# Building the block Toeplitz matrix of a state-space mixer with selecting matmuls and ScalarE copies instead of on-chip transfers

## The chip, the cores and the metric

One core of one Trainium2 chip runs the whole program. The metric is device time in microseconds (us), the median over several executions. The granted TensorE clock has two levels, 2.4 GHz ("1.00" in the profile) and 1.2 GHz ("0.50").

## What is computed

One inference step of a two-layer decoder trunk over 512 prompt tokens and 8 sample tokens, width 1024, all in float32. Layer 0 is a diagonal complex state-space mixer (S5) and a mixture of 16384 tiny experts (PEER); layer 1 is latent attention and a second PEER. What matters here is the mixer and the modulation vectors:

```
mod = silu(c) @ w_mod + b_mod              # 9 rows of c, 16384 columns in all: 64 MB of weights
h   = rmsnorm(x) * (1 + scale) + shift
bu[l] = h[l] @ b_bar;  s[l] = lam_bar * s[l-1] + bu[l]      # 64 groups, 64 states, 16 inputs each
y[l]  = real(c_mat @ s[l]) + d_skip * h[l]
```

The recurrence is cut into 64 chunks of 8 tokens. Inside a chunk, y is a product of the chunk's inputs with a block Toeplitz matrix: for each of the 64 groups a 128 x 128 matrix whose block (s, t), 16 x 16, is the response K[t-s] of the group for t >= s, and zero for t < s. Between chunks only the state is carried.

## The kernel before

**The weight blocks.** `w_mod` is read in 32 blocks of 2 MB (numbers 0 to 31), each as two halves of 1 MB and a bias row of 2 KB, all issued by the SP queue (`mod_loads`, L785 and L787). A block has one of two slots (its number's parity, called b). The load of block n+2 into a slot is issued half by half, as TensorE finishes each half of block n (`s_modmm`). TensorE multiplies a block in `mod_pair` (L2469, 64 instructions; L2474 with the bias, 8), which waits for the whole block; ScalarE copies the 9 x 512 result out of PSUM (`mod_copy`, L1214, four pieces) and stores it to `mod_rows` in HBM.

**The rounds.** TensorE goes through a fixed list, `ROUNDS`: m (turns the input tables), s (turns the sample rows), u (turns the prompt rows), i (injections into the states), k (the responses: 16 groups each, into PSUM), y (the output). The 8 PSUM banks are two halves; a round waits until the round before it in its half was copied out. `MOD_AFTER` says after which round one weight block each is multiplied. Blocks 0 to 3 come before all rounds (`MOD_FIRST = 4`), 4 to 21 between them, and 22 to 31 after k3 in a loop of their own, with other places in SBUF (`MOD_ONE = 22`, `MOD_PLACES[1]`). Their load waits until round k3 is multiplied (`s_mm`). SP loads blocks 0 to 5 without regard to the rounds, then waits for the stored rows of blocks 0 to 3, reads these back, and goes on with block 6.

**The Toeplitz matrix.** `toep` lies where `MOD_PLACES[0]` lay, so it waits for block 21. GpSimd clears it (L1107, 128 x 8192) and then issues 32 transfers from SBUF to SBUF (L1112): for each of the 4 k rounds and each s of 8, the copied responses `ksb[r]` (16 partitions at partition 32r, 16 groups x 128 columns) go to partitions 16s to 16s+15, shifted right by 16s columns:

```
for s in range(TC):
    pool.dma_start(toep[GP * s:GP * (s + 1), RG * r:RG * (r + 1), GP * s:P],
                   ksb[r][:, :, 0:P - GP * s]).then_inc(s_toep, 16)
```

In all 2.36 MB, in 8192 contiguous pieces of 512 down to 64 bytes.

**After it.** VectorE copies the i rounds out (L1836 to L1841), then runs the scan over the chunks (up to L1913). When the scan, block 31 and the 32 transfers are done, VectorE (L1918) and ScalarE (L1284) place the states in `hx`, two copies each, and TensorE does the y rounds (L2535, L2536). The GLU, PEER, attention and the second PEER follow, with waits only on work of their own. GpSimd's gathers of expert rows (L1124) are the long part of the program.

Of the kernel before, what the change touches and what calls it, by code (L numbers as in the profile page):

```python
# [12 lines left out]
ACT = mybir.ActivationFunctionType  # L13
AX = mybir.AxisListType

P = 128
# [4 lines left out]
NB = 8  # L21
# [32 lines left out]
MOD_S5 = 4  # L54
MOD_FIRST = 4
MOD_ONE = 22
HALF_MOD = KD * MB // 2


def program(nc, a):  # L60

    with ExitStack() as ctx:
# [29 lines left out]
        SEL = o; o += NB  # L92
        EYE = o; o += 32
        SILU = o; o += KD * NC9
# [117 lines left out]
        s_tz = sem("chunk_pad_and_response_cleared")  # L212
        s_toep = sem("response_loaded")
        s_mm = sem("s5_round_products")
# [35 lines left out]
        def row_no(passes, stage, j):  # L250
# [3 lines left out]
                    if row_slot(q, m) == slot and not (passes is LOADS and (q, m) in NOT_LOADED)]  # L254
# [4 lines left out]
                  + [("i", 0), ("k", 0), ("m", 2), ("i", 1), ("k", 1), ("m", 3), ("i", 2), ("k", 2), ("i", 3), ("k", 3)]  # L259
                  + [("y", r) for r in range(NR)])  # L260
        WHO = {"u": "A", "k": "A", "m": "A", "i": "V", "s": "A", "y": "V"}
        MOD_AFTER = [("m", 0), ("m", 1), ("m", 1), ("s", 0), ("u", 0), ("u", 1), ("u", 2), ("u", 3), ("u", 3), ("k", 0),
                     ("m", 2), ("i", 1), ("k", 1), ("m", 3), ("i", 2), ("k", 2), ("i", 3), ("k", 3)]
        assert MOD_FIRST + len(MOD_AFTER) == MOD_ONE
        round_no = {key: n for n, key in enumerate(ROUNDS)}
# [500 lines left out]
        def _(sp):  # L766
            sp.dma_start(at(SILU, KD * NC9), a["c_t"]).then_inc(s_in, 16)
            sp.dma_start(at(IDENT, P + TOPK + NB + 32), a["consts"]).then_inc(s_in, 16)
            sp.dma_start(par, a["s5_par"][:, 0:NPAB]).then_inc(s_par, 16)
# [37 lines left out]
            for b in range(2):  # L807
                sp.wait_ge(s_modmm[b], NMB)
            sp.wait_ge(s_toep, 16 * TC * NR)
            sp.dma_start(hx[:, :, CH:CH + NB], a["state_x"]).then_inc(s_st0, 16)  # L810
# [285 lines left out]
        def _(pool):  # L1096
# [8 lines left out]
            for b in range(2):  # L1105
                pool.wait_ge(s_modmm[b], MOD_ONE)
            pool.memset(at(TOEP, G * P), 0.0).then_inc(s_tz, 1)  # L1107
            pool.wait_ge(s_tz, 3)
            for r in range(NR):
                wait_copied(pool, ("k", r))  # L1110
                for s in range(TC):
                    pool.dma_start(toep[GP * s:GP * (s + 1), RG * r:RG * (r + 1), GP * s:P],  # L1112
                                   ksb[r][:, :, 0:P - GP * s]).then_inc(s_toep, 16)

# [65 lines left out]
        def _(act):  # L1180
# [55 lines left out]
            act.wait_ge(s_ms, 1)  # L1236
            act.activation(stat[:, 8:13], stat[:, 8:13], ACT.Sqrt).then_inc(s_rt, 1)

            for key in ROUNDS[:round_no[("y", 0)]]:
                kind, r = key  # L1240
                if WHO[kind] == "V":
                    for pair in mods_between(key):
                        mod_copy(*pair, one=True)
                    continue
                act.wait_ge(s_mm, round_no[key] + 1)
                ps = half(key)
                if kind == "u":
                    for s in range(2):
                        ins = act.activation(
                            u2[64 * s:64 * s + 64, RG * r:RG * (r + 1), 0:CH].rearrange(  # L1250
                                "p (b g) c -> p b g c", b=4),
                            ps[0:64].rearrange("p b (g c) -> p b g c", g=4)[:, :, :, 64 * s:64 * s + 64], ACT.Copy)
                        if s == 0:
                            link(ins)
                elif kind == "s":
                    act.wait_ge(s_tz, 1)
                    turned = ps[:, 0:2].rearrange("p b n -> p (b n)")
                    link(act.activation(u2[0:GP, :, CH:CH + NB], turned[0:GP, NB * (TC - 1):NB * (TC - 1 + G)].rearrange(
                        "p (g b) -> p g b", g=G), ACT.Copy))
                    ins = act.activation(u2[96:P, :, CH + NB:UC], turned[96:P, 0:NB * G].rearrange(  # L1260
                        "p (g b) -> p g b", g=G), ACT.Copy)
                elif kind == "k":
                    ins = act.activation(ksb[r].rearrange("p (b g) m -> p b (g m)", b=4), ps[0:GP], ACT.Copy)
                else:
                    if r >= 2:
                        act.wait_ge(s_mm, round_no[("i", r - 2)] + 1)
                    if r == 0:
                        act.wait_ge(s_blp, 3)
                        act.wait_ge(s_lam, 16)
                    ins = act.activation(minb[r % 2].rearrange("p (b g) m -> p b (g m)", b=4), ps, ACT.Copy)  # L1270
                ins.then_inc(s_evA, 1)
                for pair in mods_between(key):
                    mod_copy(*pair, one=True)
                if kind == "s":
                    act.wait_ge(s_cn, 1)
                    act.activation(cl[0:64, :, 0, :], c_re[0:64], ACT.Copy).then_inc(s_clr, 1)
                    act.activation(cl[64:P, :, 0, :], c_im[64:P], ACT.Copy, scale=-1.0).then_inc(s_clr, 1)
            mod_evac(MOD_ONE, NMB)

            act.wait_ge(s_scd, 1)  # L1280
            act.wait_ge(s_modmm[1], NMB)
            act.wait_ge(s_toep, 16 * TC * NR)
            for gp in range(2):
# [379 lines left out]
        def _(dve):  # L1663
# [251 lines left out]
            dve.wait_ge(s_modmm[1], NMB)  # L1915
            dve.wait_ge(s_toep, 16 * TC * NR)
            for gp in range(2):
# [539 lines left out]
        def _(pe):  # L2457
# [22 lines left out]
            def mod_products(first, last, places):  # L2480
                pairs(pe, first, last, mod_pair(places))

            pe.wait_ge(s_silu, 2)
            pe.wait_ge(s_const, 1)
            mod_products(0, MOD_FIRST, MOD_PLACES[0])
            for no, (kind, r) in enumerate(ROUNDS):
                key = kind, r
                if round_before(no):
                    wait_copied(pe, round_before(no))
# [4 lines left out]
                if kind == "s":  # L2494
# [5 lines left out]
                    for pair in mods_between(key):  # L2500
                        mod_pair(MOD_PLACES[0], True)(*pair)
                    continue
                if key == ("k", 0):
                    pe.wait_ge(s_clr, 3)
# [5 lines left out]
                if kind == "y" and r == 0:  # L2510
                    wait_copied(pe, ("i", NR - 1))
                    mod_products(MOD_ONE, NMB, MOD_PLACES[1])
                    for b in range(2):
                        pe.wait_ge(s_modev[b], 2 * NMB)
                    pe.wait_ge(s_hx, 4)
                    pe.wait_ge(s_st0, 16)
                    pe.wait_ge(s_toep, 16 * TC * NR)
                for gl in range(RG):
# [547 lines left out]
def host_inputs(i):  # L3066
# [6 lines left out]
    arr["consts"] = np.concatenate([np.eye(P), np.tile(np.arange(TOPK), (P, 1)),  # L3073
                                    np.arange(P)[:, None] // 16 == np.arange(NB)[None],
                                    np.arange(P)[:, None] % 32 == np.arange(32)[None]], 1).astype(np.float32)
# [68 lines left out]
```

## Time and profile before

| | us |
|---|---|
| median of 3 executions | 3530.94 (3530.49 to 3539.13) |
| the profiled execution, its own time | 3527.4 |
| its span, first to last instruction | 3525.6 |
| first y round starts | 272.70 |
| granted TensorE clock over the span | 0.790 |

All times below count from the start of the span. In the timeline a row is: start, duration, engine, line, operation, output and input, count, and in brackets how long the engine had been idle and what ended it. SPq is the SP queue issuing transfers. TensorE shows each float32 matmul of the program as two instructions.

### The profile page before, as it was taken

The numbers are of one execution on the slowest core, as the hardware profiler recorded it, in microseconds if no ns is written. First come the engines' busy times: TensorE is split into PE (matmuls) and PEld (weight loads), VectorE is DVE, ScalarE is ACT, GpSimd is POOL, SyncE is SP. The second block draws the span as 40 slices with busy tenths as digits, with TensorE's granted clock in tenths as the row PEclk, the third lists the DMA queues.
The fourth block names the chain that finished last, engine by engine and source line by source line (L and its number), as shares of the span: only waits on it lengthen the run. The fifth ranks groups of instructions, "written<-read, shape, count | busy, mean of one in ns | idle before, by whom it ended". The sixth has DMA issues, their size and how long they took to land.

```text
span 3525.6 us, 62302 instructions
## 1 busy us (share of the span) xinstructions
PE 2587.8 (73%) x24981; PEld 949.6 (27%) x24981; DVE 2327.5 (66%) x5468; ACT 1234.7 (35%) x3842; POOL 1261.0 (36%) x1163
## 2 busy tenths in 40 slices
PE   4857997768667766667879997686686677666666
PEld 3735523204002300112225665040040023001000
DVE  8563686986775776465544444978767767775645
ACT  3312233343333333334433232343433343333333
POOL 0020233444443444424413511344444444443432
PEclk8868998769667877769999998696696678667666
DMA  8886799999999999999952157999999999999997
GB/s 292 302 283 258 291 406 407 414 411 407 419 417 418 401 419 420 402 413 399 406 180 92 38 199 300 413 399 421 420 402 417 420 420 407 420 419 398 415 421 317
DMA packets 192059, 1278.61 MB, mean 363 GB/s; under 512 B 30904, under 2 KB 36704, under 8 KB 44760
## 3 DMA queue, kind: packets, MB, share of 16 engines
q0 software_dynamic: 152912, 1112.35, 77.3%
q1 hardware_dynamic: 38288, 161.79, 12.7%
q8 instruction: 191, 3.13, 0.4%
q14 instruction: 92, 0.75, 0.1%
q10 hardware_dynamic: 576, 0.59, 0.1%
HBM read 1260.88 MB, written 11.40 MB: 361 GB/s over the span
## 4 chain that ended last, share of the span: by engine, by line
DMA 39%; PE 37%; DVE 16%; ACT 5%; issue 3%; POOL 0%; SPq 0%; ACTq 0%; DVEq 0%; PEldq 0%; POOLq 0%
DMA arena<-peer_uv,arena 35%; PE psum L2677 12%; DVE arena L2106 8%; PE psum L2622 6%; PE psum L2583 3%; DMA arena<-b_mod 2%; PE psum L3042 2%; PE psum L2756 1%; PE psum L2825 1%; PE psum L2469 1%; ACT arena L1397 1%; ACT arena L1394 1%; DVE arena L2024 1%; DVE arena L2117 1%; DVE arena L1679 1%
## 5 line engine op out<-in xcount | busy, mean ns | idle before, releaser
L2677 PE MATMUL psum<-arena 32*32 32x512 f32 x16384 | 1520.5, 815 | 743.9 <-ACT arena L1397 727.4
L1124 POOL DMA_INDIRECT arena<-peer_uv,arena x1040 | 1141.9, 1098 | 1825.8 <-PE psum L2677 1542.8
L2106 DVE SCALAR_TENSOR_TENSOR arena<-arena 128x1024 f32<-128x1024 f32 x1040 | 1273.4, 1226 | 757.3 <-DMA arena<-peer_uv,arena 740.0
L1384 ACT ACTIVATE arena<-arena 128x1 f32<-128x1 f32 x1040 | 210.4, 202 | 1551.0 <-DVE arena L2106 1550.1
L2677 PEld LDWEIGHTS psum<-arena 32*32 32x32 f32 x16384 | 216.0, 118 | 1907.5 <-ACT arena L1397 1783.5
L1397 ACT ACTIVATE arena<-arena 128x32 f32<-128x32 f32 x1024 | 329.1, 321 | 33.4
L1394 ACT ACTIVATE arena<-arena 128x1 f32<-128x1 f32 x1040 | 306.0, 294 | 33.8
L2622 PE MATMUL psum<-arena 128*128 128x128 f32 x2048 | 262.7, 285 | 14.8 <-DMA arena<-peer_wq 13.7
L2622 PEld LDWEIGHTS psum<-arena 128*128 128x128 f32 x2048 | 244.7, 197 | 83.6 <-issue 82.1
L2469 PE MATMUL psum<-arena 128*9 128x128 f32 x2048 | 87.5, 341 | 85.1 <-DMA arena<-b_mod 85.1
L2583 PE MATMUL psum<-arena 128*128 128x512 f32 x256 | 124.4, 618 | 2.9 <-DVE arena L1931 2.1
L1145 POOL TENSOR_SCALAR arena<-arena 128x128 f32<-128x128 f32 (+3 forms) x64 | 68.9, 1085 | 91.6 <-DVE arena L2329 91.5
L1679 DVE TENSOR_TENSOR arena<-arena 128x512 f32<-128x512 f32 (+9 forms) x177 | 89.3, 505 | 9.3 <-ACT arena L1192 2.6
L2469 PEld LDWEIGHTS psum<-arena 128*9 128x9 f32 x2048 | 64.1, 111 | 105.0 <-issue 52.2
L2106 DVE DVE_READ_ACCUMULATOR arena<-arena 128x1 f32 x1040 | 85.6, 82 | 0.0
L1214 ACT ACTIVATE arena<-psum 9x128 f32<-9x128 f32 x128 | 34.5, 269 | 129.2 <-PE psum L2474 126.9
L2024 DVE MAX8 arena<-arena 128x8 f32<-128x128 f32 (+1 forms) x204 | 61.9, 331 | 17.5 <-ACT arena L1354 15.1
L1603 ACT ACTIVATE arena<-psum,arena 128x128 f32<-128x128 f32 (+3 forms) x64 | 33.8, 528 | 103.8 <-DVE arena L2324 103.1
L2583 PEld LDWEIGHTS psum<-arena 128*128 128x128 f32 x256 | 45.2, 192 | 81.5 <-issue 74.8
L2024 DVE FIND_INDEX8 arena<-arena 128x8 uint32<-128x128 f32 (+1 forms) x204 | 65.6, 329 | 0.0
L2026 DVE FIND_INDEX8 arena<-arena 128x8 uint32<-128x128 f32 (+1 forms) x204 | 65.5, 329 | 0.0
L2025 DVE MATCH_REPLACE8 arena<-arena 128x128 f32<-128x128 f32 (+1 forms) x204 | 64.3, 320 | 0.0
(341 smaller groups left out, 2292.3 us busy)
## 6 DMA issues: line engine op xcount, KB each, us to landing
arena<-w_mod SPq DMA_DIRECT2D x64, 1024.0 KB
arena<-peer_wq SPq DMA_DIRECT2D x12, 2048.0 KB
arena<-peer_uv,arena POOLq DMA_INDIRECT x1040
arena<-w_glu SPq DMA_DIRECT2D x5, 2048.0 KB, 12.3
arena<-mod_rows SPq DMA_DIRECT2D x4, 1024.0 KB
arena<-w_o SPq DMA_DIRECT2D x1, 4096.0 KB
arena<-mod_rows SPq DMA_DIRECT2D x7, 512.0 KB
arena<-x_after_layer SPq DMA_DIRECT2D x7, 512.0 KB
```

Of the source, the lines that this page charges most:

```text
L1124: pool.indirect_dma_start(ring[r], None, a[f"peer_uv{t // 5}"], bass.IndirectOffsetOnAxis(ap=ix, axis=0)).then_inc(landed[r], 16)
L1384: act.activation(col, col, ACT.Gelu_apprx_tanh).then_inc(s_gl, 1)
L1394: act.activation(wcol, col, ACT.Copy, scale=gate_).then_inc(s_gl, 1)
L1397: act.activation(diag[:, n_ % RING, :], eye32, ACT.Copy, scale=wcol).then_inc(s_dg, 1)
L1679: link(dve.tensor_tensor(out, x, y, op))
L2024: steps = (lambda x, v, i: dve.max(v[:, 0:8], x), lambda x, v, i: dve.max_index(i[:, 0:8], v[:, 0:8], x), lambda x, v, i: dve.match_replac ...
L2106: dve.scalar_tensor_tensor(out=u, in0=u, scalar=1.0, in1=h, op0=ALU.mult, op1=ALU.mult, accum_out=at(DOTS + (t % 2) * 2 * P + m, 1)).then_ ...
L2469: ins = pe.matmul(mod_bank(b, q, one), silu[:, k, :], w[k // 4][:, k % 4, MQ4 * q:MQ4 * (q + 1)], start=(k == 0), stop=False, skip_group_c ...
L2583: ins = pe.matmul(psum[:, unit_bank(u), :], ztk[:, k, P * j:P * (j + 1)], w[:, k, :], start=(k == 0), stop=(k == KD - 1))
L2622: ins = pe.matmul(psum[:, 4 + m % 2, P * q:P * q + R], (wq[:, m, k] if t else wide(WQ0[m])[:, k])[:, P * q:P * (q + 1)], htr[:, k, 0:R], s ...
L2677: ins = pe.matmul(acc_of(t, i, c), diag[rows, r, :], ring[r][rows, D + 512 * c:D + 512 * (c + 1)], start=(m == 0), stop=last, skip_group_c ...
L3042: ins = pe.matmul(psum[:, 5 + n_, :], ot[:, k, :], wo[:, k, 512 * n_:512 * (n_ + 1)], start=(k == 0), stop=(k == KD - 1))
```

## The change

The 32 transfers go. The list of rounds gets four t rounds between k3 and the y rounds. A t round r handles groups 4n to 4n+3 of each of the four `ksb` (n = r): for each 32 output partitions c, an even and an odd 16-row block is produced by a matmul whose stationary operand is a 16 x 32 piece of an identity (one piece gives rows 0 to 15, the other, shifted by 16 zero columns, rows 16 to 31), both accumulated in PSUM. ScalarE then copies four pieces into `toep`. GpSimd only clears the three strips below the block diagonal.

Blocks 4 and 5 are multiplied before the rounds (`MOD_FIRST = 6`), so one block less lies after m1 and one less after u3. Blocks 22 to 25 use the old places and don't wait for k3's products; they are multiplied ahead of t0. Blocks 26 to 31 come in pairs behind t0, t1 and t2, in the other places.

```
-MOD_FIRST = 4
-MOD_ONE = 22
+MOD_FIRST = 6
+MOD_ROUNDS = 22
+MOD_ONE = 26
...
+                  + [("t", r) for r in range(NR)] + [("y", r) for r in range(NR)])
...
-        MOD_AFTER = [("m", 0), ("m", 1), ("m", 1), ("s", 0), ("u", 0), ("u", 1), ("u", 2), ("u", 3), ("u", 3), ("k", 0),
+        MOD_AFTER = [("m", 0), ("m", 1), ("s", 0), ("u", 0), ("u", 1), ("u", 2), ("u", 3), ("k", 0),
                      ("m", 2), ("i", 1), ("k", 1), ("m", 3), ("i", 2), ("k", 2), ("i", 3), ("k", 3)]
...
# SP
-            sp.wait_ge(s_toep, 16 * TC * NR)
+            wait_copied(sp, ("t", NR - 1))
# GpSimd
-            pool.memset(at(TOEP, G * P), 0.0).then_inc(s_tz, 1)
-            pool.wait_ge(s_tz, 3)
-            for r in range(NR):
-                wait_copied(pool, ("k", r))
-                for s in range(TC):
-                    pool.dma_start(toep[GP * s:GP * (s + 1), RG * r:RG * (r + 1), GP * s:P],
-                                   ksb[r][:, :, 0:P - GP * s]).then_inc(s_toep, 16)
+            for c in range(1, 4):
+                pool.memset(toep[32 * c:32 * c + 32, :, 0:32 * c], 0.0).then_inc(s_tz, 1)
# ScalarE
+            mod_evac(MOD_S5, MOD_FIRST)
...
+                if key == ("t", 0):
+                    mod_evac(MOD_ROUNDS, MOD_ONE)
+                    for b in range(2):
+                        act.wait_ge(s_modmm[b], MOD_ONE)
...
+                elif kind == "t":
+                    out = toep.rearrange("p (r g) m -> p r g m", r=NR)
+                    src = ps.rearrange("p r (g m) -> p r g m", g=4)
+                    for c in range(4):
+                        rows, t0 = slice(32 * c, 32 * c + 32), 32 * c
+                        ins = act.activation(out[rows, :, 4 * r:4 * r + 4, t0:P], src[rows, :, :, t0:P], ACT.Copy)
+                        if c < 3:
+                            link(ins)
...
+                if kind == "t" and MOD_ONE + 2 * r < NMB:
+                    for b in range(2):
+                        mod_copy(MOD_ONE // 2 + r, b)
...
-            mod_evac(MOD_ONE, NMB)
-            act.wait_ge(s_toep, 16 * TC * NR)
+            wait_copied(act, ("t", NR - 1))
# TensorE
+            def responses(ps, n_):
+                for c in range(4):
+                    for odd in range(2):
+                        t0 = GP * (2 * c + odd)
+                        for r in range(NR):
+                            out = ps[32 * c:32 * c + 32, r, :].rearrange("p (g m) -> p g m", g=4)
+                            ins = pe.matmul(out[:, :, t0:P], at(EYE - GP * odd, 32, 32 * r, 32 * r + GP),
+                                            ksb[r][:, 4 * n_:4 * n_ + 4, 0:P - t0], start=(odd == 0), stop=(odd == 1),
+                                            skip_group_check=True)
+                ins.then_inc(s_mm, 1)
...
+                if key == ("t", 0):
+                    wait_copied(pe, ("i", NR - 1))
+                    mod_products(MOD_ROUNDS, MOD_ONE, MOD_PLACES[0])
...
+                if kind == "t":
+                    responses(ps, r)
+                    if MOD_ONE + 2 * r < NMB:
+                        for b in range(2):
+                            mod_pair(MOD_PLACES[1])(MOD_ONE // 2 + r, b)
+                    continue
...
-                    mod_products(MOD_ONE, NMB, MOD_PLACES[1])
...
-                    pe.wait_ge(s_toep, 16 * TC * NR)
+                    pe.wait_ge(s_tz, 5)
```

## Rows read from the trace of the kernel before

**Rows 1.** Who waited for whom, 0 to 420 us: total, times, longest.
```profile
PE psum L2469 <- DMA arena<-b_mod: 85.1, 19, 27.0
DVE arena L1918 <- PE psum L2474: 31.0, 1, 31.0
```
**Rows 2.** Timeline, end of the scan to the first y round.
```profile
231.89 0.43 DVE L1913 TENSOR_TENSOR arena<-arena 128x256 f32<-128x256 f32 x1
...
259.06 3.60 PE L2469 MATMUL psum<-arena 128*9 128x128 f32 x64 [3.65 <-DMA arena<-b_mod]
262.60 0.61 PE L2474 MATMUL psum<-arena 1*9 1x128 f32 x8
263.27 3.81 DVE L1918 COPY arena<-arena 64x2048 f32<-64x2048 f32 x2 [30.96 <-PE psum L2474]
...
265.20 7.30 ACT L1284 ACTIVATE arena<-arena 64x2048 f32<-64x2048 f32 x2 [0.71 <-ACT arena L1214]
...
272.70 0.67 PE L2535 MATMUL psum<-arena 128*72 128x128 f32 x2 [9.49 <-ACT arena L1284]
```
**Rows 3.** Stretches: busy us of the engines, granted clock, DMA share, GB/s.
```profile
191.60:237.40 45.80, 20.71 (x360) 12.57 (x360) 38.99 (x90) 5.39 (x20) 17.67 (x33) 0.50 1.02 285
237.40:259.10 21.70, 12.23 (x292) 8.54 (x296) 0.00 (x0) 4.31 (x16) 0.00 (x0) 0.81 0.94 359
```
**Rows 4.** The 32 transfers of the responses, all instructions of L1112.
```profile
L1112 POOL DMA_DIRECT2D arena<-arena x32: 511/564/597, 191.9 to 209.0; - x32
...
DMA to landing us min/median/max: 5.2/16.4/29.6
```
**Rows 5.** Timeline, 45 to 80 us: loads of early blocks and first rounds.
```profile
45.70 1.97 SPq L785 DMA_DIRECT2D arena<-w_mod  x2
...
54.66 0.34 SPq L797 DMA_DIRECT2D arena<-mod_rows  x1
...
62.18 3.65 PE L2528 MATMUL psum<-arena 128*128 128x128 f32 x16 [15.03 <-DVE arena L1783]
...
67.50 1.56 SPq L785 DMA_DIRECT2D arena<-w_mod  x2
...
77.33 0.95 POOL L1100 MEMSET arena<- 128x1024 f32 x1 [76.47 <-DVE arena L1804]
...
79.25 7.64 PEld L2497 LDWEIGHTS psum<-arena 8*128 8x128 f32 x71 [0.42 <-issue]
```
**Rows 6.** Timeline, blocks 11 and 12 and round i0.
```profile
109.93 1.93 PE L2469 MATMUL psum<-arena 128*9 128x128 f32 x64 [1.38 <-DMA arena<-b_mod]
...
111.79 0.40 PE L2474 MATMUL psum<-arena 1*9 1x128 f32 x8
...
119.68 7.12 PE L2531 MATMUL psum<-arena 128*128 128x80 f32 x32
```
**Rows 7.** Timeline, blocks 20 and 21 and the load of block 22.
```profile
176.60 1.93 PE L2469 MATMUL psum<-arena 128*9 128x128 f32 x64
...
182.09 0.29 PE L2469 MATMUL psum<-arena 128*9 128x128 f32 x3
...
182.82 1.85 SPq L785 DMA_DIRECT2D arena<-w_mod  x2
```
**Rows 8.** Timeline, blocks 22 and 27, and the load of block 31.
```profile
191.59 3.60 PE L2469 MATMUL psum<-arena 128*9 128x128 f32 x64 [7.05 <-DMA arena<-b_mod]
...
237.42 3.58 PE L2469 MATMUL psum<-arena 128*9 128x128 f32 x64 [4.97 <-DMA arena<-b_mod]
...
250.10 2.16 SPq L785 DMA_DIRECT2D arena<-w_mod  x2
```
**Rows 9.** ScalarE, groups by shape, 0 to 300 us: count, busy us, mean ns.
```profile
L1214 ACT ACTIVATE arena<-psum 9x128 f32<-9x128 f32 x128 | 34.5, 269 | 129.2 <-PE psum L2474 126.9
L1249 ACT ACTIVATE arena<-psum 64x1024 f32<-64x1024 f32 x8 | 8.1, 1017 | 3.4 <-PE psum L2522 3.2
...
L1263 ACT ACTIVATE arena<-psum 16x2048 f32<-16x2048 f32 x4 | 7.5, 1866 | 17.2 <-PE psum L2525 17.2
```
**Rows 10.** TensorE's timeline in the expert stage: matmuls on four row groups in turn.
```profile
446.93 1.09 PE L2677 MATMUL psum<-arena 32*32 32x512 f32 x16 [0.20 <-ACT arena L1397]
```

More of the change, by code:

```diff
@@ L92, in program @@
         SEL = o; o += NB
-        EYE = o; o += 32
+        EYE = o + GP; o += GP + 32
         SILU = o; o += KD * NC9
@@ L212, in program @@
         s_tz = sem("chunk_pad_and_response_cleared")
-        s_toep = sem("response_loaded")
         s_mm = sem("s5_round_products")
@@ L259, in program @@
                   + [("i", 0), ("k", 0), ("m", 2), ("i", 1), ("k", 1), ("m", 3), ("i", 2), ("k", 2), ("i", 3), ("k", 3)]
-                  + [("y", r) for r in range(NR)])
-        WHO = {"u": "A", "k": "A", "m": "A", "i": "V", "s": "A", "y": "V"}
-        MOD_AFTER = [("m", 0), ("m", 1), ("m", 1), ("s", 0), ("u", 0), ("u", 1), ("u", 2), ("u", 3), ("u", 3), ("k", 0),
+                  + [("t", r) for r in range(NR)] + [("y", r) for r in range(NR)])
+        WHO = {"u": "A", "k": "A", "m": "A", "i": "V", "s": "A", "t": "A", "y": "V"}
+        MOD_AFTER = [("m", 0), ("m", 1), ("s", 0), ("u", 0), ("u", 1), ("u", 2), ("u", 3), ("k", 0),
                      ("m", 2), ("i", 1), ("k", 1), ("m", 3), ("i", 2), ("k", 2), ("i", 3), ("k", 3)]
-        assert MOD_FIRST + len(MOD_AFTER) == MOD_ONE
+        assert MOD_FIRST + len(MOD_AFTER) == MOD_ROUNDS
         round_no = {key: n for n, key in enumerate(ROUNDS)}
@@ L767, in _ @@
             sp.dma_start(at(SILU, KD * NC9), a["c_t"]).then_inc(s_in, 16)
-            sp.dma_start(at(IDENT, P + TOPK + NB + 32), a["consts"]).then_inc(s_in, 16)
+            sp.dma_start(at(IDENT, P + TOPK + NB + GP + 32), a["consts"]).then_inc(s_in, 16)
             sp.dma_start(par, a["s5_par"][:, 0:NPAB]).then_inc(s_par, 16)
@@ L1915, in _ @@
             dve.wait_ge(s_modmm[1], NMB)
-            dve.wait_ge(s_toep, 16 * TC * NR)
+            wait_copied(dve, ("t", NR - 1))
             for gp in range(2):
@@ L2510, in _ @@
                 if kind == "y" and r == 0:
-                    wait_copied(pe, ("i", NR - 1))
-                    mod_products(MOD_ONE, NMB, MOD_PLACES[1])
                     for b in range(2):
@@ L3073, in host_inputs @@
     arr["consts"] = np.concatenate([np.eye(P), np.tile(np.arange(TOPK), (P, 1)),
-                                    np.arange(P)[:, None] // 16 == np.arange(NB)[None],
+                                    np.arange(P)[:, None] // 16 == np.arange(NB)[None], np.zeros((P, GP)),
                                     np.arange(P)[:, None] % 32 == np.arange(32)[None]], 1).astype(np.float32)
```

## The prediction

> **What bounds the kernel now.** I read the list of waits first. In the first 420 us TensorE's largest wait is for the weight blocks, 85.1 us, and VectorE stands still once for 31.0 us until the last block is multiplied [rows 1]. So the mixer stage ends with the stream of weight blocks, not with the scan: the timeline has the scan's last step at 232.3, block 31 multiplied at 263.2, ScalarE's two state copies from 265.2 to 272.5, and the first y round at 272.7 [rows 2]. Everything after that is in an unchanged order and waits only for work that starts after this point, so what the change is worth is how far that 272.7 moves. I take the 3250 us behind it as shifted whole.
>
> Next the stream itself, by stretches. From 191.6 to 237.4 the DMA engines are full (share 1.02) yet move only 285 GB/s; from 237.4 to 259.1 they move 359 at a share of 0.94 [rows 3]. The difference is the 32 on-chip transfers, issued from 191.9 to 209.6 and landing up to 29.6 us later, thus by about 230 [rows 4]. Blocks 22 to 27 start at 191.6 and 237.4, five intervals of 9.2 us; blocks 27 to 31 at 237.4 and 259.1, four intervals of 5.4 us [rows 2, 8].
>
> **The early rounds: earlier by 9.4 us.** TensorE is idle for 15.0 us before round m0, which waits for a VectorE table until 62.2 [rows 5]. Blocks 4 and 5 now go there. Block 5's load was issued at 45.7 [rows 5]; from first issue to start block 31 took 259.1 - 250.1 = 9.0 and block 22 took 191.6 - 182.8 = 8.8 [rows 2, 7, 8], so I use 8.9: block 5 is ready at 54.6 and, at 4.2 us for a block at 1.2 GHz (3.60 + 0.61, [rows 2]), done at 58.8. The idle time covers both blocks; without the cover they'd cost 8.4. ScalarE's two sets of copies (four of 0.27 us, [rows 9]) lie in its wait for m0. SP goes on to block 6 right behind the reads that begin at 54.7, instead of at 67.5 [rows 5], so blocks 6 and 7 are in time behind m0 and m1.
>
> Round s0 then waits only for VectorE, which released GpSimd's memset at 77.3; before it started at 79.3, behind block 6 [rows 5]: 1.9 us gained. Between s0 and i0 lie five blocks now, not six. What was block 11, with its wait, was done at 111.8 + 0.4 = 112.2, and i0 started at 119.7 behind block 12 [rows 6]. The slot of block 11 becomes that of block 12, i0 starts at 112.2 - 1.9 = 110.3: 9.4 earlier. From there to k3 the sequence is the same. I let it all move by 9.4. Bounds: 1.9 if the block left out is only waited for elsewhere, and 9.4; nothing excludes a small loss if the clock falls in the new gap before s0, but the 9.4 already keeps low-clock durations of those rounds. The value taken is the upper one, because each piece behind s0 has its predecessor in the old order with the same waits.
>
> **The stream starts 14.6 us earlier.** Block 20 started at 176.6; its first half is done 1.0 later, 177.6. Block 22's load waited for k3 and was issued at 182.8 [rows 7]. It now needs only block 20's half: 177.6 - 9.4 = 168.2, which is 14.6 earlier. Block 22 is ready at 168.2 + 8.9 = 177.1, and the i3 copies, which TensorE also awaits, are no later than that (block 22 was multiplied long after them).
>
> **The transfers go: 18.8 us.** The five intervals take 45.8 us; at 5.4 each they'd take 27.0. So -18.8 [rows 2, 8]. Bounds: the bytes alone, 2.36 MB at the 0.41 MB/us that 2 MB in about 5.1 us makes, would be 5.8 us; the whole excess is 18.8. I take the excess, as the full DMA share with fewer bytes says that the engines were busy on small pieces [rows 3].
>
> The Trainium skill speaks against that value: its page DMA: Bandwidth & Descriptors, section "Why small descriptors are slow (HBM only)", says that transfers from SBUF to SBUF don't suffer the penalty of small pieces. By it the gain here would be 5.8 and not 18.8; the rows seem to disagree, and the case stands below as a rival.
>
> **What the t rounds cost.** *Products.* A t round has 4 x 2 x 4 = 32 matmuls, 64 instructions, over 8 widths (512, 448, ... 64 columns). The four of one width use four row groups and four banks, as in the expert stage, where 16 such instructions of 512 columns take 1.09 us, 0.27 per four [rows 10]. The four widest groups by columns: (512+448+384+320)/512 x 0.27 = 0.88; the four narrow ones by count, 16 at 0.030 (1.93 us for 64, [rows 6]): 0.48; twice, for the two passes: 2.7 us at 2.4 GHz. At 1.2 GHz, 1.76 and 16 x 0.056 (3.60 for 64, [rows 2]), twice: 5.3. In the quiet stretch the clock was mixed, 0.81 [rows 3]; TensorE now has more to do there, so 3.5 us. If nothing overlapped, 64 instructions would have 18432 columns in a row: 9.7 us, or 19.4 at 1.2 GHz.
>
> *Copies.* From 1.02 us for 1024 elements and 1.87 for 2048 [rows 9], 0.83 ns per element and 0.17 fixed: pieces of 2048, 1536, 1024 and 512 give 1.87 + 1.44 + 1.02 + 0.59 = 4.9, with the links 5.1 us.
>
> *Where they lie.* Walking two blocks and a round at a time, with 3.4 us for a block between its 2.3 and 4.2: blocks 22 to 25 start at 177.1, 182.6, 187.7 and 193.3; t0 takes until 200.2; blocks 26 and 27 until 207.3; t1 until 210.8; 28 and 29 until 217.9; t2 until 221.4; 30 and 31 until 228.5. Block 31's data is ready at 225.1, 34.0 before the 259.1 of before. That agrees with 14.6 + 18.8 = 33.4: t0 to t2 fit between the arrivals of blocks (3.4 + 3.4 + 3.5 against 10.8 for two arrivals), and ScalarE's 5.1 for a round and 2.2 for two blocks also fit in 10.8. Behind block 31 lie open: t3, +3.5; its copies, +5.1; less the 2.0 which ScalarE formerly took from block 31's end to its state copies, and 0.8 from the shorter block. The state copies stay, 7.3 [rows 2]. They are the next thing queued on ScalarE behind t3; VectorE now waits for t3's copies too, but its 3.8 end before ScalarE's.
>
> The scan, moved by 9.4 with i3, ends at 222.9 and is hidden by 14 us. GpSimd's three memsets clear 12288 elements per partition; at 0.95 us for 1024 [rows 5] that is 11.4 us behind block 25, near 208 and long before y0. The load of the sample states (SP, behind t3) is in the shade of the state copies as before.
>
> **The sum.** -14.6 - 18.8 + 3.5 + 5.1 - 2.0 - 0.8 = -27.6. The first y round starts at 245.1. The profiled execution took 3527.4 (span 3525.6 and 1.8 around it): 3499.8. The median lies 3.5 above it: 3503.3.
>
> **Rivals.**
> (a) *TensorE stays at 1.2 GHz* as in the stretch from 191.6 to 237.4 [rows 3]. For it: the waits for blocks remain at first. Against it: TensorE was busy 45% there and would be at nearly 100% here. Then from block 25's end at 197.6 TensorE is never idle: 4 x 5.3 + 6 x 4.2 = 46.4, 5.1, 7.3, 0.3: y0 at 256.7, -16, 3515.
> (b) *The transfers cost only their bytes* and 13.0 us of the slow intervals have another cause which stays: -27.6 + 13.0 = -14.6, 3516. For it: that stretch also has the low clock. Against it: the intervals shorten as the last transfers land. This is the case that the Trainium skill's section named above would give.
> (c) *The early gain is given back* at s0 or by waits for blocks between the rounds, so that k3 is 1.9 earlier only: -20.1, 3511. For it: the DMA share is high there. Against it: SP restarts 11 us earlier.
> (d) *Slower: the products of a t round don't overlap, at 1.2 GHz.* 197.6 + 4 x 19.4 + 25.2 + 12.7 = 313.1: +40, 3571. It decides from (272.7 - 197.6 - 25.2 - 12.7) / 4 = 9.3 us per round. For it: 16 rows, not 32, and widths that change. Against it: row groups and banks are laid out as in [rows 10]. Without overlap but at 2.4 GHz it would be about -10, 3521.
> (e) *The chain doesn't move*: the expert stage, bound by its own gathers, takes up the gain: 0, 3531. I see no wait in it for a fixed time.
>
> **The numbers.** Forecast 0.70; (a) 0.08, (b) 0.06, (c) 0.07, (d) 0.04 slow and 0.02 at full clock, (e) 0.03. At full clock throughout the forecast would be about -32. The range 3496 to 3518 takes in the forecast, (a), (b) and (c). Within 0.3% (10.6 us, about what a measurement of this kernel can tell) of no change lie (e) and half the fast form of (d); slower is (d).
>
> **What would show it.** i0 at 110.3; block 22's load issued at 168 and 5.4 us between blocks; a t round of 2.7 to 5.3 us, its copies 5.1; y0 at 245; no transfer from SBUF to SBUF. If a t round takes more than 9, or blocks 22 to 25 still come every 9 us, the prediction is wrong.

## The result, and the profile after

The changed kernel takes 3478.64 us (median of 4, 3471.24 to 3482.64) against 3530.72 on the same chip (median of 4): a ratio of 0.9848, 95% interval 0.982 to 0.9875. That is 52 us less where 27.6 were forecast, outside the stated range of 3496 to 3518. The profiled execution took 3471.24, its span is 3469.1.

The mixer goes nearly as forecast. TensorE's waits for weight blocks, from the list of waits of the changed kernel, 0 to 420 us (compare [rows 1]):

```profile
PE psum L2479 <- DMA arena<-b_mod: 63.1, 21, 28.0
```

TensorE's timeline of the changed kernel: m0, i0, block 22 (against [rows 5 to 8]):

```profile
62.49 2.79 PE L2557 MATMUL psum<-arena 128*128 128x128 f32 x16 [2.15 <-DVE arena L1793]
...
110.53 3.80 PE L2560 MATMUL psum<-arena 128*128 128x80 f32 x32
...
169.17 3.60 PE L2479 MATMUL psum<-arena 128*9 128x128 f32 x64 [2.73 <-DMA arena<-b_mod]
```

TensorE's idle time ahead of m0 shrank from 15.0 to 2.2 us: blocks 4 and 5 are in it. i0 starts at 110.5 (110.3 forecast), and runs at full clock, 3.80 us where it had taken 7.12. Block 22 starts at 169.2, not 177.1.

The timeline from block 31 to the first y round (against [rows 2]); L2500 are the products of round t3, L1260 its copies on ScalarE:

```profile
222.34 3.60 PE L2479 MATMUL psum<-arena 128*9 128x128 f32 x64 [3.78 <-DMA arena<-b_mod]
...
226.27 2.90 PE L2500 MATMUL psum<-arena 16*32 16x512 f32 x61
...
229.27 5.01 ACT L1260 ACTIVATE arena<-psum 32x2048 f32<-32x2048 f32 x4 [1.50 <-PE psum L2500]
...
234.38 4.01 DVE L1928 COPY arena<-arena 64x2048 f32<-64x2048 f32 x2 [20.14 <-ACT arena L1260]
234.39 7.50 ACT L1294 ACTIVATE arena<-arena 64x2048 f32<-64x2048 f32 x2
...
242.25 0.67 PE L2564 MATMUL psum<-arena 128*72 128x128 f32 x2 [13.08 <-ACT arena L1294]
```

The first y round starts at 242.3 instead of 272.7, 30.4 earlier (27.6 forecast). But the span shrank by 56.5. The other 26 us lie behind the first y round, where the program was thought unchanged. The gathers of expert rows show where: GpSimd's instructions of the gather line, first of the kernel before, then of the changed one (count, shortest/median/longest ns, first and last start):

```profile
L1124 POOL DMA_INDIRECT arena<-peer_uv,arena x1040: 934/939/2033, 373.5 to 3496.0; - x174
```

```profile
L1119 POOL DMA_INDIRECT arena<-peer_uv,arena x1040: 935/939/2086, 345.4 to 3439.3; - x174
```

From first to last gather 3122.5 us before and 3093.9 after: 28.6 less. (From the first y round to the first gather it was 100.8 us before and 103.2 after, 2.4 more.) Taken every 16 gathers, the lead of the changed kernel grows steadily (28 at the first, 34 at the 256th, 41 at the 512th), stands still through the attention, and grows to 57 at the last. A stretch of 400 us in the gathers, before and after (columns as in [rows 3]):

```profile
800.00:1200.00 400.00, 298.46 (x3069) 100.73 (x3067) 277.23 (x665) 142.79 (x490) 169.78 (x156) 0.77 1.01 412
```

```profile
800.00:1200.00 400.00, 292.73 (x2980) 85.29 (x2976) 287.86 (x703) 143.69 (x496) 171.44 (x159) 0.75 1.01 419
```

The DMA engines are full in both (share 1.01), and move 419 GB/s instead of 412. So each row came in a little faster, and the cause must be one that reaches there.

### The profile page after: what moved, and what is told of

Same layout as the page of the kernel before. It is cut to its first block, busy times and chain, and to the rows that moved or that the text cites. A ratio compares the mean times of both kernels' runs of the same rounds, so it can differ in the third digit from the quotient of the medians.

```text
span 3469.1 us, 62774 instructions
## 1 busy us (share of the span) xinstructions
PE 2581.9 (74%) x25237; PEld 946.9 (27%) x25237; DVE 2326.7 (67%) x5468; ACT 1255.2 (36%) x3858; POOL 1240.5 (36%) x1133
## 4 chain that ended last, share of the span: by engine, by line
DMA 37%; PE 37%; DVE 17%; ACT 5%; issue 3%; POOL 0%; SPq 0%; DVEq 0%; ACTq 0%; PEldq 0%; POOLq 0%
DMA arena<-peer_uv,arena 34%; PE psum L2706 12%; DVE arena L2116 9%; PE psum L2651 7%; PE psum L2612 3%; DMA arena<-b_mod 2%; PE psum L3071 2%; PE psum L2854 1%; PE psum L2785 1%; ACT arena L1407 1%; ACT arena L1404 1%; DVE arena L2034 1%; DVE arena L2127 1%; PE psum L2479 1%; DVE arena L1689 1%
## 5 line engine op out<-in xcount | busy, mean ns | idle before, releaser
L1140 POOL TENSOR_SCALAR arena<-arena 128x128 f32<-128x128 f32 (+3 forms) x64 | 68.9, 1085 | 91.6 <-DVE arena L2339 91.5
L2034 DVE MAX8 arena<-arena 128x8 f32<-128x128 f32 (+1 forms) x204 | 61.9, 331 | 18.3 <-ACT arena L1364 15.9
```

The costliest lines, as they stand in the source:

```text
L2034: steps = (lambda x, v, i: dve.max(v[:, 0:8], x), lambda x, v, i: dve.max_index(i[:, 0:8], v[:, 0:8], x), lambda x, v, i: dve.match_replac ...
```

## The experiments

Three theories for the faster gathers, and chance as the fourth. **S:** the 16 columns which the change adds to the constants move everything behind them in SBUF by 64 bytes, the ring of expert rows too. **T:** the 32 transfers leave something on GpSimd's queue. **H:** the wider array of constants moves the expert tables in HBM. **V:** executions differ.

**1. The shift alone.**

```
-        EYE = o; o += 32                 # the kernel before
+        EYE = o; o += 32 + 16
```

> The kernel before, with 16 unused words per partition put behind the identity pieces in SBUF, so that everything behind them (the ring of expert rows too) starts 64 bytes later, as in the changed kernel; nothing else. The ring then starts at byte 82304 of the kernel's SBUF tensor instead of 82240 (a multiple of 128 instead of only 64). Theory S (where the gathered rows land in SBUF sets the rate of the gathers): first y round at 272.7 as before, but from the first to the last expert gather about 28 us less than the 3122.5 of before, so about 3505. Theory T (the 32 transfers on GpSimd's queue leave something behind that slows the later gathers), theory H (the wider constants move the expert tables in HBM), and theory V (executions differ by chance): no change, 3531 within 6.

Measured: 3500.29 against 3526.18, ratio 0.9923 (0.9899 to 0.9946). Its gathers and the same stretch:

```profile
L1124 POOL DMA_INDIRECT arena<-peer_uv,arena x1040: 932/937/1981, 368.8 to 3469.4; - x174
...
800.00:1200.00 400.00, 299.40 (x3088) 97.49 (x3096) 284.23 (x691) 145.29 (x500) 173.24 (x159) 0.77 1.01 419
```

3100.6 us from first to last, 419 GB/s, with all 32 transfers in place. An edit of one number that computes nothing is worth 26 us: 22 between the gathers, and the first y round of this profile lies 5.6 earlier, of which more below.

**2. The array wider in HBM alone.**

```
-    [... eye32], 1)                      # host array of the kernel before
+    [... eye32, np.zeros((P, 16))], 1)
-            sp.dma_start(..., a["consts"])
+            sp.dma_start(..., a["consts"][:, 0:P + TOPK + NB + 32])
```

> The kernel before, with the array of constants 16 columns wider in HBM only; these are not loaded and SBUF is laid out as before. Theory H (the expert tables' place in HBM sets the rate of the gathers): about 28 us less from first to last gather, so about 3505. Theories S, T and V: no change, 3531 within 6.

Measured: 3525.61 against 3526.18, ratio 0.9996 (0.9978 to 1.0013), 3130.8 us from first to last gather. H falls:

```profile
L1124 POOL DMA_INDIRECT arena<-peer_uv,arena x1040: 935/939/2082, 370.0 to 3500.8; - x174
```

**3. No transfers.**

```
-            for r in range(NR):          # the kernel before
-                wait_copied(pool, ("k", r))
-                for s in range(TC):
-                    pool.dma_start(toep[...], ksb[r][...]).then_inc(s_toep, 16)
-            ...wait_ge(s_toep, 16 * TC * NR)
+            ...wait_ge(s_tz, 3)          # four places
```

> The kernel before without its 32 transfers from SBUF to SBUF (the Toeplitz matrix stays zero, so that part of the mixer's output is left out); the waits for them become a wait for the clearing. All theories of the mixer: the weight blocks 22 to 31 come every 5.4 us, block 22 at about 191, so block 31 at about 240 and the first y round at about 254 (18.8 us earlier than 272.7). If the transfers cost only their bytes: about 267. Behind that, theory T wants the gathers 28 us faster in sum (about 3484 in all), theories S, H and V no change there (about 3512).

Measured: 3509.56 against 3526.18, ratio 0.9953 (0.9933 to 0.9973). From first to last gather 3132.7 us: T falls. In the mixer, blocks 22 and 31 and the first y round:

```profile
181.18 3.24 PE L2464 MATMUL psum<-arena 128*9 128x128 f32 x64 [6.84 <-DMA arena<-b_mod]
...
234.33 2.91 PE L2464 MATMUL psum<-arena 128*9 128x128 f32 x64 [1.78 <-DMA arena<-b_mod]
...
247.27 0.67 PE L2530 MATMUL psum<-arena 128*72 128x128 f32 x2 [9.49 <-ACT arena L1279]
```

Nine intervals take 53.1 us, 5.9 each; with the transfers they took 67.5 in the kernel before and 68.9 in the mean of the five profiles of that mixer (experiments 1, 2, 6, 13 and the kernel before). So the transfers cost the stream 15.8 us. The first y round is 19.8 us earlier than the mean of those five, 267.1 (267.1, 266.8, 267.9, 260.8, 272.7), but 3.9 of these lie ahead of the start of block 22 (185.1 in the mean, 181.2 here) and are not the transfers'. The bytes of the transfers alone would have made 5.8.

The DMA records show where the time goes. The transfers' own packets, from 194.9 to 238.1 us in the kernel before, took 9.3 us of all 16 engines. In the same stretch the weights' packets of 8 KB took 474 ns in the mean, against 351 between 182 and 226 us here: 1144 packets, 123 ns more each, over 16 engines, are another 8.8 us. (The two together are more than 15.8, as the engines were not quite full here: share 0.96 against 1.02.) So about half of what the transfers cost was paid by the weights' packets beside them.

**4. The changed kernel at the old places.** The constants in another order, so that the shifted pieces of the identity borrow 16 zero columns of the full identity; no column more.

```
-        IOTA = o; o += TOPK              # the changed kernel
-        SEL = o; o += NB
-        EYE = o + GP; o += GP + 32
+        EYE = o; o += 32
+        IOTA = o; o += TOPK
+        SEL = o; o += NB
```

> The changed kernel with its constants in another order, so that the shifted pieces of the identity need no 16 further columns: the constants are as wide as before and everything behind them in SBUF is back at the old places. The mixer is the changed one: first y round at about 242. Theories S and H: the gathers are as slow as before, 3122 us from first to last, so about 3503 in all, near what was predicted. Theories T and V: as the changed kernel, about 3478.

Measured: 3509.01 against 3526.18, ratio 0.995 (0.993 to 0.9969); first y round at 240.6, 3132.4 from first to last gather. So this is the change without its accident: 17 us faster (11 to 25 by the interval), not 52.

**5. Another place: 128 bytes below the fast one.**

```
-        ONES = o; o += 16                # the kernel of experiment 4
+        ONES = ARENA - 16
```

> The changed kernel with the constants reordered (no 16 further columns) and the 16 words of ones moved to the end of SBUF, so that the ring of expert rows starts at byte 82176 of the tensor, a multiple of 256 (82304 in the changed kernel, a multiple of 128; 82240 before, of 64). If what matters is that the rows' pieces start at multiples of 128 bytes: 8 KB packets at a flat 309 ns, first to last gather about 3095 to 3100 us, in all like the changed kernel, within 6. If 256 brings more: packets under 309 ns and a total some us below 3475.

Measured: 3506.03 against 3522.62, ratio 0.9952 (0.9932 to 0.9971). The place was a multiple of 256 within the tensor and yet slow, 3122.5 us from first to last gather. It is also a second measurement of the change at a slow place: 16.6 us faster. My reading "multiples of 128 within the tensor" fell.

**6. 32 bytes below.**

```
-        EYE = o; o += 32                 # the kernel before
+        EYE = o; o += 32 + 8
```

> The kernel before with everything behind the identity pieces 32 bytes later: the ring at byte 82272, a multiple of 32 only. Theory S with a dependence on the alignment: at least as slow as before, packets of 8 KB at a median of 312 ns or more, first to last gather 3122 us or more, in all 3526 or more. If only the place (some bank or port at that address) and not the alignment counts: something between before and the shift by 64 bytes, 3500 to 3526.

Measured: 3534.08 against 3522.62, ratio 1.0025 (1.0005 to 1.0045), 3134.0 between the gathers. At least as slow as before: not a matter of nearness.

**7. The early blocks undone in the changed kernel.**

```
-MOD_FIRST = 6
+MOD_FIRST = 4
-        MOD_AFTER = [("m", 0), ("m", 1), ("s", 0), ("u", 0), ("u", 1), ("u", 2), ("u", 3), ("k", 0),
+        MOD_AFTER = [("m", 0), ("m", 1), ("m", 1), ("s", 0), ("u", 0), ("u", 1), ("u", 2), ("u", 3), ("u", 3), ("k", 0),
```

> The changed kernel with the first part undone: four blocks before the rounds, two each behind m1 and u3, as before. My prediction's term: the first y round 9.4 us later than in the changed kernel, about 252 against 242, in all about 9 more. The rival (c) of the prediction: about 2 later only.

Measured: 3483.24 against 3522.62, ratio 0.988 (0.9845 to 0.9915). In its timeline i0 starts at 120.5 and the first y round at 254.0, 10 and 12 us behind the changed kernel. The ratios of the two kernels, 0.988 here and 0.985 to 0.986 for the changed one, can't be told apart.

**8. The products of a t round row group by row group.**

```
-                for c in range(4):
-                    for odd in range(2):
-                        t0 = GP * (2 * c + odd)
-                        for r in range(NR):
+                for r in range(NR):
+                    for c in range(4):
+                        for odd in range(2):
+                            t0 = GP * (2 * c + odd)
```

> The changed kernel with the products of a t round in another order: all eight of one row group in a row, then the next, so that no two neighbours use different row groups. If the matmuls overlap only between row groups: a t round of about 10 us instead of 3 (at full clock), the first y round 7 us later by the last round and up to 20 by all four, 249 to 262. If they did not overlap in the changed kernel either: no change.

Measured: 3479.65 against 3522.62, ratio 0.987 (0.9835 to 0.9904), first y round at 238.5:

```profile
196.90 3.70 PE L2500 MATMUL psum<-arena 16*32 16x512 f32 x64
```

A t round takes 3.7 us, twice, at a granted clock of 1.00, then 4.4 and 4.0 at 0.82 and 0.90. The changed kernel's take 3.2, 2.6, 2.9 and 3.3, at 0.80, 1.00, 0.88 and 0.80. At the full clock the order is worth 1.1 us a round, not the 7 I expected. The 18432 columns in a row would take 9.7 us by the prediction's estimate, so the matmuls of one row group overlap too; which of them do is not shown.

**9. The changed kernel again,** beside experiments 10 to 12.

> The changed kernel once more, unchanged, beside the other three on one chip. If the two parts of the gain found so far hold: first y round near 242, first to last gather near 3095, 8 KB packets at 309 ns, about 48 below the kernel before. If part of the gain was chance, it shows here as a smaller difference.

Measured: 3476.21 against 3526.79, ratio 0.9861 (0.9839 to 0.9882); first y round at 241.8, 3100.3 between the gathers. Not chance: the eleven profiled kernels with the ring at a fast place have 3093.9 to 3106.8 between the gathers and one outlier, experiment 8, with 3119.3; the six at a slow place have 3122.5 to 3134.0. (In experiment 8 96% of the 8 KB packets took 309 ns too; where its 19 us went is open.)

**10. 256 bytes below the fast place.**

```
-        STAT = o; o += 64                # the kernel of experiment 4
+        STAT = ARENA - 64
+        o += 16
```

> The changed kernel with the constants reordered and the 64 words of statistics moved to the end of SBUF, so that the ring starts at byte 82048 of the tensor: 256 bytes below the fast place 82304. The three slow places (82240, 82176, 82272) lie 64, 128 and 32 bytes from it. If multiples of 256 bytes (from the fast place) are what counts: 309 ns flat, first to last gather about 3095, in all as the changed kernel. If multiples of 512: slow, packets at 311 to 313 at the median and about 3125, in all about 28 more.

Measured: 3480.14 against 3526.79, ratio 0.985 (0.982 to 0.9879). Fast again:

```profile
L1120 POOL DMA_INDIRECT arena<-peer_uv,arena x1040: 932/937/2101, 348.8 to 3447.6; - x174
```

The gather packets of 8 KB (one row each), from the DMA records of the traces; the place is the ring's first byte within the kernel's SBUF tensor:

```
kernel            place   from 82304   share at 309 ns   5%/median/95% ns   mean ns   first to last gather us
before            82240      -64            0.24           309/312/320       319.2        3122.5
experiment 4      82240      -64            0.26           309/312/320       319.9        3132.4
experiment 5      82176     -128            0.45           309/311/321       318.8        3122.5
experiment 6      82272      -32            0.22           309/313/321       320.3        3134.0
experiment 10     82048     -256            0.97           309/309/309       315.8        3098.8
experiment 1      82304        0            0.96           309/309/309       316.0        3100.6
after             82304        0            0.97           309/309/309       315.2        3093.9
```

133120 packets, 4.0 ns less each between before and after, over 16 engines: 33 us, against the 28.6 measured.

**11. Block 22 waits for k3 again.**

```
-            mod_loads(MOD_S5 + 2, MOD_ONE, MOD_PLACES[0])
+            mod_loads(MOD_S5 + 2, MOD_ROUNDS, MOD_PLACES[0])
+            sp.wait_ge(s_mm, round_no[("k", NR - 1)] + 1)
+            mod_loads(MOD_ROUNDS, MOD_ONE, MOD_PLACES[0])
```

> The changed kernel, where the load of block 22 waits again until round k3 is multiplied; the places in SBUF stay the new ones. My prediction's term for this wait is 5.2 us: the first y round at about 247 instead of 242, in all about 5 more. If the stream is bound elsewhere, no change.

Measured: 3478.93 against 3526.79, ratio 0.9864 (0.9837 to 0.9892). The load starts at 161.9, right behind k3, and not at 155.2 as in experiment 9; block 22 starts 5.3 us later than there, as the term says. The nine intervals then take 52.6 instead of 55.2, and the first y round comes at 244.5, 2.7 later: less than builds of one order differ among themselves (239.8 to 249.0). In the total nothing is to be seen.

**12. A try at a better version: VectorE places all the states.**

```
-            wait_copied(dve, ("t", NR - 1))
-            for gp in range(2):
-                dve.tensor_copy(hxv[64:P, gp], hpv[64 * gp:64 * gp + 64, 1]).then_inc(s_hx, 1)
+            dve.wait_ge(s_mm, round_no[("t", NR - 1)] + 1)
+            for k in range(2):
+                for gp in range(2):
+                    dve.tensor_copy(hxv[64 * k:64 * k + 64, gp], hpv[64 * gp:64 * gp + 64, k]).then_inc(s_hx, 1)
...
-            wait_copied(sp, ("t", NR - 1))
+            sp.wait_ge(s_mm, round_no[("t", NR - 1)] + 1)
```

> An attempt at a better version: VectorE does all four copies of the states and starts when round t3 is multiplied, not when its copies are done; SP loads the sample states from the same point. So ScalarE's last copies (5.0 us) and the state copies (four of 1.9 us) run side by side. Expected: state copies from about 229 to 237, first y round at about 237 instead of 242, in all 5 us less than the changed kernel. If the copies of both engines slow one another, or the sample states land late, less.

Measured: 3477.71 against 3526.79, ratio 0.9857 (0.9835 to 0.9878). Its timeline does what was meant:

```profile
226.74 5.01 ACT L1260 ACTIVATE arena<-psum 32x2048 f32<-32x2048 f32 x4 [0.88 <-PE psum L2499]
...
226.81 7.64 DVE L1927 COPY arena<-arena 64x2048 f32<-64x2048 f32 x4 [15.54 <-PE psum L2499]
...
234.81 0.67 PE L2563 MATMUL psum<-arena 128*72 128x128 f32 x2 [8.17 <-DVE arena L1927]
```

From the start of ScalarE's last copies to the first y round it takes 8.1 us instead of 13.0: 4.9 saved, as expected. (That the first y round is 7 us earlier than in experiment 9 has to do with a t3 at the full clock too, 2.6 us instead of 4.7.) But the total is no lower than experiment 9's 3476.21. It is not shown to beat the changed kernel.

**13 to 15. The mixer in three steps, all at the fast places.** The kernel of experiment 1 as the base; the base with the early blocks alone; the changed kernel.

```
-MOD_FIRST = 4                            # step of 14 on 13; MOD_AFTER as in the changed kernel
+MOD_FIRST = 6
+            mod_evac(MOD_S5, MOD_FIRST)  # ScalarE, before the rounds
```

> The base of this group: the kernel before with everything behind the identity pieces 64 bytes later (as in the first experiment). Expected about 26 below the kernel before, first y round about 267.

> That base with the first part of the change alone: blocks 4 and 5 before the rounds, transfers and the rest as before. By my prediction's term i0 and all behind it start 9.4 earlier, so the total is 9 below the base. If the gain is given back in the stream with the transfers (which then begin earlier too, beside the same loads), 0 to 5.

> The changed kernel in the same group. Against the base only the mixer differs: by the first y rounds seen so far (267 and 242 to 249) 18 to 25 below the base; by the total of the changed kernel with the old places, 17; by the prediction's sum, 27.6.

Measured, against 3527.14 for the kernel before: 3503.14 (ratio 0.9934, 0.9911 to 0.9957), 3487.79 (0.9884, 0.9864 to 0.9905), 3480.29 (0.9862, 0.9837 to 0.9888). The first y rounds: 260.8, 253.3, 239.8. So the places in SBUF bring 24.0 us, the early blocks 15.4 more, the t rounds in the transfers' place 7.5 more: 46.9. The single steps have an uncertainty of some 8 us each, and the profiles share the mixer's gain otherwise (7.5 and 13.5); the mixer's sum is 22.9 by the medians and 21.0 by the profiles. These three profiles are the fairest to compare, as in all of them TensorE's granted clock was 1.00 from i0 to k3.

## Why the prediction was wrong

**The step that failed** is the first part's last sentence, "I take the 3250 us behind it as shifted whole". The front part of the diff makes the constants 16 columns wider. I gave that edit no price. It moves every tile behind it by 64 bytes, among them the ring into which 1.09 GB of expert rows are gathered, by DMA engines that are full (share 1.01) in the stretches shown. At the new place 97% of the 8 KB packets take 309 ns; at the old one a quarter do. That is 24 to 26 us (experiments 1 and 13), half of the whole result, and without it the measured time would have been inside the range that I gave (experiments 4 and 5). It is shown that the place in SBUF does it, not the array in HBM (2), the transfers (3) or chance (9). All tiles moved together in these experiments; that it is the ring is read from the gather packets' own durations.

**The rule of the place.** Fast are two places 256 bytes apart; slow are those 32, 64 and 128 bytes from a fast one. The Trainium skill, page DMA: Bandwidth & Descriptors, section "How a descriptor splits into AXI transactions", says that a descriptor which starts at a multiple of 256 bytes is split into transactions of 256 bytes and a leftover, and that one which doesn't begins its first transaction at the boundary below its start. By that a row of 8192 bytes would be 32 of these when aligned and 33 when not, an estimate from the page's rule; the page words it for reads and gives no time for it. The runs agree with a period of 256. The size they don't settle: one more in 32 would be 3%, and the mean packet takes 1.3% longer (319.2 against 315.2 ns). That the tensor itself then begins 128 bytes off a boundary, and that the cut is the mechanism, is argued and not shown.

**"The early rounds: earlier by 9.4 us".** Right to the point at i0 (110.3 forecast, 110.5). Behind it more came: k3's products ended at 182.5 before and at 164.4 after, as i0 and the rounds behind it ran at the full granted clock. I had kept the low-clock durations. But that is only in part the change's doing. From i0 to k3, the kernel before and experiment 13, which has the same order:

```profile
119.70:182.40 62.70, 59.41 (x878) 51.70 (x878) 31.29 (x87) 19.05 (x41) 0.00 (x0) 0.85 0.75 274
```

```profile
117.10:169.00 51.90, 50.88 (x882) 44.57 (x879) 31.50 (x87) 19.03 (x42) 0.00 (x0) 1.00 0.88 336
```

The same rounds take 62.8 us at a granted clock of 0.85 and 51.8 at 1.00. Of the ten kernels with the early blocks eight had 1.00 there, of the seven without them one (the others 0.85 to 0.97). Rival (c), given back, did not happen. What this part is worth in the total is not well known: 15.4 by the medians of 13 and 14, 7.5 by their profiles, some 6 to 11 by the ratios of experiment 7 and the changed kernel.

**"The stream starts 14.6 us earlier".** The load of block 22 went out at 159.8 instead of 168.2. The wait for k3, for which I put 5.2, is worth 5.3 at the start of block 22 (experiment 11), half of which the intervals behind it take up, and nothing measurable in the total.

**"The transfers go: 18.8 us".** Right in kind and too large: the transfers cost 15.8 us of the stream in experiment 3, 16.6 (10 to 24) in the total. The interval left is 5.9 us, not 5.4: nine take 53.2 in the changed kernel. And the engines were busy not only "on small pieces": half of the time lies in slower packets of the weights. The last of the transfers' packets ended at 238.1, not at about 230, just where the short intervals begin. Rival (b), that they cost only their bytes, fell. The Trainium skill, page DMA: Bandwidth & Descriptors, section "Why small descriptors are slow (HBM only)", says that transfers from SBUF to SBUF don't suffer the penalty of small pieces. These runs do not agree: 2.36 MB in pieces of 64 to 512 bytes took 9.3 us of all engines in their own packets and cost the stream 15.8, where the bytes alone make 5.8. No run changed the size of the pieces.

**"What the t rounds cost".** Products 2.6 to 3.3 us (3.5 taken), copies 5.01 (5.1), the chain behind block 31 as written: 15.9 us from its last product to the first y round. My two bounds, 2.7 us at 2.4 GHz and 5.3 at 1.2, were near: rounds t0 and t1 of experiment 4 (without their first three instructions), the first at a granted clock of 0.50, the second at 1.00, take 4.7 and 2.6 us in all:

```profile
188.64 4.37 PE L2500 MATMUL psum<-arena 16*32 16x512 f32 x61
...
199.29 2.42 PE L2500 MATMUL psum<-arena 16*32 16x512 f32 x61
```

Rivals (a) and (d), a low clock throughout and no overlap, fell: the clock from block 22 to block 31 was 0.76 (0.66 to 0.78 in the six kernels with the whole changed mixer), and even in the worse order a round takes 3.7 to 4.4. Rival (e), that the expert stage takes the gain up, did not come true, though its own rate changed, for another reason.

**The sum.** The mixer's 27.6 was too high by some 4 us. By the medians it is 22.9 at a fast place (15 less 13) and 17.2 and 16.6 at the old place and at 82176 (4, 5), each uncertain by some 7 to 12. By the profiles, the means of the five kernels with the old mixer (before, 1, 2, 6, 13) and of the six with the whole changed one (after, 4, 5, 9, 10, 15):

```
                               old mixer   changed   gained   forecast
start of i0                        119.1     110.2      8.9        9.4
load of block 22 goes out          176.5     159.7     16.8       14.6
start of block 22                  185.1     169.3     15.8       14.6
nine intervals, 22 to 31            68.9      54.4     14.5       18.8
block 31 to the first y round       13.1      20.0     -6.9       -5.8
start of the first y round         267.1     243.7     23.4       27.6
```

So inside the mixer the mis-sized term is the interval that is left without the transfers: 5.9 to 6.0 us where I took 5.4. The first y round of 245.1 that I forecast was within 2 us of the mean, in part by luck: my base, the one profile with 272.7, was 5.6 later than the mean, and the gain 4.2 too large. Builds that order the mixer alike differ by some 10 us, and most of it goes with the granted clock between i0 and k3: the changed mixers start their first y round at 239.8 to 242.3 when it was 1.00 and at 248.4 and 249.0 when it was 0.90 and 0.91; the old ones at 260.8 when it was 1.00, at 266.8 to 267.9 at 0.90 to 0.97 and at 272.7 at 0.85. What decides which clock a build gets there is open.

## What to carry to other kernels

Ask of every edit what it moves, not only what it does: a tile that grows shifts all that are laid out behind it, and where a queue of large transfers is the bound, its target's place modulo 256 bytes can matter (0.7% of this program); try a few places before crediting the rest of the change. Compare the first and the last milestone of the part that was edited, and of the part that wasn't, before explaining a total. Many small transfers on chip can take more time from full DMA engines than their bytes say (15.8 us against 5.8 here), in part by slowing the packets beside them. Copies by matmul and ScalarE beside a stream of loads were nearly free here except for the last round: the nine intervals took 54.4 us with them in the mean and 53.1 with neither them nor the transfers. And compare with more than one profile of the kernel before: this one was the latest of five.

## What the runs showed of the hardware

- Gather packets of 8 KB into SBUF: 309 ns for 96 to 97% of them at two places 256 bytes apart; 311 to 313 at the median, up to 321 (95%), at three places 32, 64 and 128 bytes off. From 800 to 1200 us the full DMA engines (share 1.01) moved 416 to 419 GB/s at these two places and 409 to 414 at the other three.
- 32 transfers from SBUF to SBUF, 8192 small pieces (2.36 MB), beside a full stream: 15.8 us of the stream. Their packets took 9.3 us of all engines, and the weights' packets of 8 KB beside them 474 ns in the mean instead of 351.
- Float32 matmuls of 16 rows and 32 columns, 64 to 512 wide: a round of 64 instructions takes 2.6 us at a granted clock of 1.00 and 4.7 at 0.50 when neighbours change the row group, 3.7 at 1.00 when they keep it.
- Four ScalarE copies of PSUM (32 partitions, 2048 to 512 elements): 5.01 us, the same when VectorE copies in SBUF beside them.
